# Hybrid attention and gMLP block on one core: the split of two turned blocks one step up, and the product with the gate on VectorE

## The chip, the cores and the metric

The kernel runs on one core of one Trainium2 chip. The metric is the device time of one execution in microseconds (us); the number compared is the median of several runs. Besides the runs there is one profiled execution, from which all rows below are taken. PE is the matrix engine (TensorE), PEld its weight load, ACT is ScalarE, DVE is VectorE, POOL is GpSimd, and SP is the engine that issues most of the DMAs.

## The reference

One layer of a decoder trunk over 1024 positions of width 1024, in float32:

```python
h      = rms_norm(x, pre_norm)
proj   = h @ w_in            # q, k, v, gate_a, u_b, v_b, gate_b, mg_a, mg_b
o_a    = sliding_window_attention(q, k, v, sinks, rel_bias)   # 16 heads of 64, 2 kv heads, window 128
y_a    = (o_a * silu(gate_a)) @ w_branch_a
o_b    = spatial_gating(gelu(u_b), gelu(v_b), ...)            # chunks of 128
y_b    = (o_b * silu(gate_b)) @ w_branch_b
merged = sigmoid(mg_a) * y_a + sigmoid(mg_b) * y_b
x      = x + rms_norm(merged @ w_out, post_norm)
```

The change concerns `o_a * silu(gate_a)`. In `sliding_window_attention` each block of 128 queries attends the 128 keys of its own block up to the diagonal and the keys of the block before it above the diagonal. With a sink the softmax has one more column, which is dropped afterwards.

## The kernel before, in words

**Matrix products.** Every float32 product is made of three products of rounded operands: high half by high half, high half by low half, low half by high half. The high half is a rounding copy (ACT writes it), the low half is the value minus the high half (POOL or DVE). The projection of `h` goes through 24 pairs `n` of 128-column slices of `w_in`: pairs 0 to 15 are in turn a Q pair (a slice of q and the slice of gate_a that belongs to it) and an M pair (merge gates), pairs 16 to 23 are U pairs. Each pair is computed by a seven-product scheme (products 1 to 7 of quarters); a product is 12 matmuls of 128x512. The order is written out by hand: pair `n` has seven steps `s`, and in step `s` PE runs the product `STEPS[s]` of (2, 6, 7, 5, 1, 3, 4), where product 1 is already that of pair n+1. The low halves of the weights are POOL's (`left_lo`, L1816), the high halves ACT's (`left_hi`, L1363 to L1382), four sums per pair are POOL's too (L1881 to L1890). ACT copies the products 1, 6 and 5 out of PSUM (L1396, L1408, L1422, semaphore `ev_ok`); products 6, 5 and 3 of the same bank wait for these copies.

**Attention between the products.** A pair `p` of heads (8 in all) is spread over 22 steps, k = 0 to 21, where k = 7(n-1)+s - 14p; the next pair of heads begins 14 steps after the one before, so its steps 0 to 7 coincide with the steps 14 to 21 of the one before. `attention_all(n, s)` lists, for the current step, first the older pair of heads and then the newer. Each engine has its own loop over n and s and calls `attend(p, k)` for these; PE does so in the middle of its product, after 6 of the 12 matmuls, the others ahead of the step's other work (`after(n, s)`).

Eight blocks of 128 queries start at steps 0, 1, 3, 4, 6, 7, 9, 10: scores on PE (L1049), mask, bias and maximum on DVE (L2131, L2134), exponentials on ACT (L1572), a step later division on ACT (L1580) and a turn of 32x32 squares on DVE (L2143). Two blocks make a couple c = 0 to 3. `couple_at(k, lag)` gives the couple with 3c + lag = k:

- lag 3, SP: `prob_away` stores the probabilities of the couple in DRAM (L665), behind the turn.
- lag 5, SP: `prob_back` loads them back turned as a whole, in four DMAs (L673), behind the store (`prob_out`) and behind POOL's low half of the couple before (`pool_own`, L671), because there is one buffer `turned_in`.
- lag 7, ACT, behind the step's other work: `turned_hi` copies the high half into `pt_pack` (L1589). It waits for the four loads (`prob_in`) and for the values of the couple before (`values_ok`).
- lag 8, POOL, ahead of the step's other work: low half (L1859), then the mask that makes `pt_prev` (L1864, `pt_ok`).
- lag 9, PE: `values` multiplies with v into a half of `ps_m` (L1072), behind `pt_ok` and `oadd_ok` of two couples before. In this step the values stand ahead of the scores.
- lag 10, ACT and DVE: ACT copies one half of the heads' values to the other partitions (L1604, L1605), DVE adds the other half to it in `o_tmp` (L2149, L2150, `oadd_ok`).
- lag 11, POOL: `o_tmp` times the gate, into the gate (L1873, `og_ok`). ACT's next copy into `o_tmp` waits for `og_ok`.
- steps 15 and 21, SP: a half of the gated rows is stored in `ga_d` (L686).

In the middle of the heads (p = 3, step 11) SP loads the k of the second kv head over the first (`load_k(1)`, L693, four DMAs). These stand in SP's queue behind `prob_back` of couple 2. PE's first scores of p = 4 wait for them (`k_in`).

After the pairs three 1024x1024 products follow (branch A, branch B, output).

Of the kernel before, what the change touches and what calls it, by code (L numbers as in the profile page):

```python
# [142 lines left out]
def build(nc, x, rel_bias, pre_norm, post_norm, w_in, sinks, sgu_ln_g, sgu_ln_b,  # L143
# [6 lines left out]
    ALU = mybir.AluOpType  # L150
# [19 lines left out]
    with ExitStack() as ctx:  # L170
# [3 lines left out]
        def sem(name):  # L174
            return ctx.enter_context(nc.semaphore(name))
# [118 lines left out]
        gt_ok, gate_ok = sem("gt_ok"), sem("gate_ok")  # L294
# [7 lines left out]
        otmp_ok, oadd_ok, og_ok = sem("otmp_ok"), sem("oadd_ok"), sem("og_ok")  # L302
# [76 lines left out]
        o_tmp = soft[:, 2 * SOFT_W + 512:2 * SOFT_W + 768]  # L379
# [3 lines left out]
        def gate_w(p, h):  # L383

            return gate[:, 0:HALF] if h == 0 else gate[:, (p % 2 + 1) * HALF:(p % 2 + 2) * HALF]
# [109 lines left out]
        def attention_all(n, s):  # L495

            k = 7 * (n - 1) + s
            p = k // 14
            last = [(p - 1, k % 14 + 14)] if 1 <= p <= HEAD_PAIRS and k % 14 + 14 < LAST_STEP else []
            return last + ([(p, k % 14)] if 0 <= k and p < HEAD_PAIRS else [])  # L500

        def blocks_at(k, lag):

            return [i for i, t in enumerate(BLOCK_AT) if t + lag == k]

        def couple_at(k, lag):

            return [j for j in range(4) if 3 * j + lag == k]

        @block.sync  # L510
        def _(sp):
# [164 lines left out]
            def attend(p, k):  # L676
                for c in couple_at(k, 3):
                    prob_away(4 * p + c)
                for c in couple_at(k, 5):
                    prob_back(4 * p + c)  # L680
                if k == 11 and p + 1 < HEAD_PAIRS:
                    load_bias(p + 1)
                if k in (15, 21):
                    h = k // 21
                    sp.wait_ge(og_ok, 4 * p + 2 * h + 2)
                    sp.dma_start(ga_d[bass.ds(p, 1), :, h * HALF:(h + 1) * HALF].rearrange("a p s -> p (a s)"),  # L686
                                 gate_w(p, h)).then_inc(ga_out[h], 16)
# [527 lines left out]
        def _(act):  # L1215
# [367 lines left out]
            def turned_hi(j):  # L1583
                act.wait_ge(prob_in, 64 * (j + 1))
                if j:
                    act.wait_ge(values_ok, 2 * j)
                else:
                    act.wait_ge(v_out, 16)
                nc.scalar.activation(pt_pack[:, 0:512], turned_in, ACT.Copy).then_inc(turn_hi, 1)  # L1589

            def attend(p, k):
                for blk in blocks_at(k, 1):
                    norm(p, blk)
                for blk in blocks_at(k, 0):
                    exps(p, blk)
                if k == 2 and p + 1 < HEAD_PAIRS:
                    act.dma_start(*skew(p + 1)).then_inc(bias_out, 16)
                for g in couple_at(k, 10):
                    gg = 4 * p + g
                    act.wait_ge(values_ok, 2 * gg + 2)  # L1600
                    if gg:
                        act.wait_ge(og_ok, gg)
                    o = ps_m[:, (g % 2) * 512:(g % 2 + 1) * 512]
                    nc.scalar.activation(o_tmp[0:64, :], o[64:128, 0:256], ACT.Copy)  # L1604
                    nc.scalar.activation(o_tmp[64:128, :], o[0:64, 256:512], ACT.Copy).then_inc(otmp_ok, 1)  # L1605

            def after(n, s):

# [73 lines left out]
            for n in range(1, PAIRS):  # L1682
                for s in range(7):
                    for at in attention_all(n, s):
                        attend(*at)
                    after(n, s)
                    for p, k in attention_all(n, s):
                        for c in couple_at(k, 7):
                            turned_hi(4 * p + c)
            def after_tile(f, i):  # L1690


# [26 lines left out]
        def _(pool):  # L1719
# [44 lines left out]
            for half in range(2):  # L1764
                c = slice(half * HALF, (half + 1) * HALF)
# [80 lines left out]
            def attend(p, k):  # L1846
                if k == 0:
                    if p:
                        pool.wait_ge(exp_ok, 8 * p)
                    else:  # L1850
                        pool.wait_ge(pool_own, 4)
                        pool.wait_ge(vlo_ok, 2)
                    nc.gpsimd.tensor_scalar(neg_s.rearrange("p (b j) -> p b j", b=2)[:, :, 0:2 * SINK_W:2 * SINK_W - 1],
                                            sink_b[:, None, 2 * p:2 * p + 2].to_broadcast([P, 2, 2]), 1.0, 1.0, ALU.mult,
                                            ALU.mult).then_inc(sink_ok, 1)
                for c in couple_at(k, 8):
                    j = 4 * p + c
                    pool.wait_ge(turn_hi, j + 1)
                    nc.gpsimd.tensor_tensor(pt_pack[:, 512:1024], turned_in, pt_pack[:, 0:512].bitcast(f32),  # L1859
                                            ALU.subtract).then_inc(pool_own, 1)  # L1860
                    pool.wait_ge(pool_own, POOL_FRONT + j + 1)
                    if j:
                        pool.wait_ge(values_ok, 2 * j)
                    nc.gpsimd.affine_select(  # L1864
                        out=pt_prev[:, :].rearrange("p (y q) -> p y q", y=8),
                        in_=pt_pack[:, :].rearrange("p (y q) -> p y q", y=8), compare_op=ALU.is_ge, fill=0.0,
                        base=-1, pattern=[[0, 8], [-1, P]], channel_multiplier=1).then_inc(pt_ok, 1)
                for g in couple_at(k, 11):
                    if g == 0:
                        pool.wait_ge(gate_ok, 2 * p + 2)  # L1870
                    part = gate_w(p, g // 2)[:, g % 2 * 256:(g % 2 + 1) * 256]
                    pool.wait_ge(oadd_ok, 4 * p + g + 1)
                    nc.gpsimd.tensor_tensor(part, o_tmp, part, ALU.mult).then_inc(og_ok, 1)  # L1873

            def left_sums_1(n):

# [53 lines left out]
        def _(dve):  # L1930
# [184 lines left out]
            def attend(p, k):  # L2115
                if k == 0:
                    if p == 0:
                        dve.wait_ge(made, MADE_BEFORE)
                    dve.wait_ge(bias_in, 16 * (p + 1))
                for blk in blocks_at(k, 1):  # L2120
                    m2 = slice(blk % 4 * 2, blk % 4 * 2 + 2)
                    dve.wait_ge(exp_ok, 8 * p + blk + 1)
                    nc.vector.reciprocal(inv_den[:, m2], row_sum[:, m2]).then_inc(inv_ok, 1)  # L2123
                for blk in blocks_at(k, 0):
                    s = 8 * p + blk
                    dve.wait_ge(scores_ok, s + 1)
                    if s >= 2:
                        dve.wait_ge(exp_ok, s - 1)
                    bank = ps_s[s % 2]
                    if blk > 0:  # L2130
                        own.link(nc.vector.copy_predicated(blocks(bank)[:, :, 1, :], before_i, blocks(bank)[:, :, 0, :]))  # L2131
                    for h in range(2):
                        bias = h * 256 + (0 if blk else P)
                        ins = nc.vector.tensor_tensor_reduce(  # L2134
                            out=neg_w(blk, h)[:, 1 - h:1 - h + P], in0=bank[:, h * 256 + P:(h + 1) * 256], in1=bias_t[:, bias:bias + P],
                            scale=-HEAD_DIM ** -0.5, scalar=sink_b[:, 2 * p + h:2 * p + h + 1], op0=ALU.add, op1=ALU.min,
                            accum_out=neg_max[:, head(blk, h)])
                    ins.then_inc(scores_used, 1)
                for blk in blocks_at(k, 1):
                    dve.wait_ge(prob_ok, 8 * p + blk + 1)  # L2140
                    for h in range(2):
                        w = prob_w(8 * p + blk, h)
                        ins = nc.vector.transpose(w, w)  # L2143
                    ins.then_inc(turn_ok, 1)
                for g in couple_at(k, 10):
                    gg = 4 * p + g
                    dve.wait_ge(otmp_ok, gg + 1)
                    o = ps_m[:, (g % 2) * 512:(g % 2 + 1) * 512]
                    own.link(nc.vector.tensor_tensor(o_tmp[0:64, :], o[0:64, 0:256], o_tmp[0:64, :], ALU.add))  # L2149
                    nc.vector.tensor_tensor(o_tmp[64:128, :], o[64:128, 256:512], o_tmp[64:128, :],  # L2150
                                            ALU.add).then_inc(oadd_ok, 1)

            def u_mix(n):

# [440 lines left out]
```

## Time and profile before

| | |
|---|---|
| median of 3 runs | 937.08 us |
| lowest and highest | 934.45, 937.41 us |
| the profiled execution | 935.18 us |
| its span, first to last instruction | 933.4 us |
| granted TensorE clock, mean | 0.997 of full speed |
| PE busy | 891.1 us |
| DVE busy | 620.2 us |
| POOL busy | 537.3 us |
| ACT busy | 507.7 us |

The span is what the trace covers; the execution's own time is 1.8 us more. The attention runs from some 150 us to 590 us. One period of 14 steps (one pair of heads) takes 50.2 us there; the pair p = 5, whose step 0 lies at 414.9 us, is the one that is followed below. Busy time alone doesn't say what sets the end: a wait that ends last does.

### The profile page before, as it was taken

Reading aid. Unit: us, or ns where it says so; the run is one execution under the profiler, and the core shown is the slowest. Engines: PE = TensorE matmul, PEld = TensorE weight load, DVE = VectorE, ACT = ScalarE, POOL = GpSimd, SP = SyncE. Lnnn points to the kernel's source line nnn. Section 1 sums busy time; section 2 is a strip of 40 time slices with the busy share of each in tenths; the row PEclk is TensorE's granted clock in tenths of the full one; section 3 lists DMA queues with packets and bytes.
Section 4 is the critical chain, followed back from the end, with each engine's and each line's share of the span. In section 5 each row is a group of like instructions: output and inputs, shape, how many; then the busy total and the mean of one; then the engine's idle time right before and its main releaser. Section 6 shows DMA issues by size and latency. Waiting matters only on the chain.

```text
span 933.4 us, 12475 instructions
## 1 busy us (share of the span) xinstructions
PE 891.1 (95%) x4204; PEld 740.2 (79%) x4204; DVE 620.2 (66%) x1135; ACT 507.7 (54%) x982; POOL 537.3 (58%) x395
## 2 busy tenths in 40 slices
PE   9999999999999998899999989999999999999997
PEld 8888888877777776677777778878888888888886
DVE  6776794544454553445454567879769968989968
ACT  6654356756757574657667674434353534434553
POOL 3564237687888776687788867645444042042226
PEclk9999999999999999999999999999999999999999
DMA  8885746444444457555444454552359560235004
GB/s 299 198 198 159 249 134 182 140 114 129 111 125 117 134 137 158 175 122 146 119 121 108 121 180 134 173 154 91 113 182 382 188 219 22 93 133 225 0 1 181
DMA packets 199184, 139.29 MB, mean 149 GB/s; under 512 B 91320, under 2 KB 164048, under 8 KB 198992
## 3 DMA queue, kind: packets, MB, share of 16 engines
q1 hardware_dynamic: 196880, 135.05, 48.7%
q10 hardware_dynamic: 2240, 3.43, 1.0%
q8 instruction: 34, 0.56, 0.3%
q14 instruction: 30, 0.25, 0.1%
HBM read 98.06 MB, written 43.54 MB: 152 GB/s over the span
## 4 chain that ended last, share of the span: by engine, by line
PE 54%; POOL 23%; issue 9%; DVE 4%; ACT 4%; DMA 3%; SPq 1%; POOLq 0%; DVEq 0%; ACTq 0%
PE acc L1032 13%; PE acc L1204 11%; PE acc L885 9%; POOL w_lo L1816 8%; PE ps_m L1204 7%; PE ps_t L1204 7%; POOL pt_pack L1859 4%; POOL pt_prev L1864 3%; DMA raw<-in_w_in 3%; PE acc L975 2%; POOL sums L1881 2%; POOL sums L1882 2%; POOL gate L1873 1%; PE ps_m L1072 1%; POOL sums L1888 1%
## 5 line engine op out<-in xcount | busy, mean ns | idle before, releaser
L1032 PE MATMUL acc<-mv,w_hi 128*128 128x512 f32 x1344 | 346.7, 391 | 1.2 <-ACT ev L1408 0.7
L1032 PEld LDWEIGHTS acc<-mv,w_hi 128*128 128x128 f32 x1344 | 247.5, 188 | 48.8 <-ACT w_hi L1363 1.1
L1032 PE MATMUL acc<-mv,w_lo 128*128 128x512 f32 x672 | 180.8, 391 | 0.0
L1816 POOL TENSOR_TENSOR w_lo<-sums,w_hi 128x1024 fp32r<-128x1024 f32 x48 | 117.2, 2444 | 71.4 <-ACT w_hi L1370 42.2
L1032 PEld LDWEIGHTS acc<-mv,w_lo 128*128 128x128 f32 x672 | 126.7, 189 | 27.5
L1816 POOL TENSOR_TENSOR w_lo<-raw,w_hi 128x1024 fp32r<-128x1024 f32 (+1 forms) x48 | 94.4, 1967 | 37.1 <-ACT w_hi L1363 27.8
L1572 ACT ACTIVATE soft<-soft,neg_max 128x129 f32<-128x129 f32 x128 | 50.5, 396 | 92.6 <-DVE neg_max L2134 68.0
L1204 PE MATMUL acc<-right,left 128*128 128x512 f32 x432 | 98.7, 389 | 0.0
L1204 PEld LDWEIGHTS acc<-right,left 128*128 128x128 f32 x432 | 81.0, 188 | 17.2 <-DVE left L2194 0.4
L1859 POOL TENSOR_TENSOR pt_pack<-soft,pt_pack 128x512 fp32r<-128x512 f32 x32 | 44.8, 1401 | 52.2 <-ACT pt_pack L1589 52.2
L885 PE MATMUL acc<-mv 128*128 128x512 f32 x288 | 69.5, 395 | 0.0
L2149 DVE TENSOR_TENSOR soft<-ps_m,soft 64x256 f32<-64x256 f32 x32 | 13.3, 417 | 84.1 <-ACT soft L1605 84.1
L1204 PE MATMUL ps_t<-right,left 128*128 128x512 f32 x288 | 67.2, 389 | 0.0
L1204 PE MATMUL ps_m<-right,left 128*128 128x512 f32 x288 | 67.2, 389 | 0.0
L1204 PEld LDWEIGHTS ps_m<-right,left 128*128 128x128 f32 x288 | 54.1, 188 | 11.2
L1204 PEld LDWEIGHTS ps_t<-right,left 128*128 128x128 f32 x288 | 54.1, 188 | 11.2
L885 PEld LDWEIGHTS acc<-mv 128*128 128x128 f32 x288 | 53.5, 189 | 11.0 <-POOL mv L1766 0.2
L2143 DVE STREAM_TRANSPOSE soft<-soft 128x128 f32<-128x128 f32 x128 | 32.3, 291 | 42.1 <-ACT soft L1580 41.9
L1580 ACT ACTIVATE soft<-soft,inv_den 128x128 f32<-128x128 f32 x128 | 44.2, 393 | 29.4 <-DVE inv_den L2123 29.3
L2131 DVE COPY_PREDICATED ps_t<-before,ps_t 128x256 f32<-128x256 int32 x56 | 24.0, 429 | 51.7 <-PE ps_t L1049 50.7
L1072 PE MATMUL ps_m<-pt_pack,v_st 128*128 128x256 f32 x128 | 26.7, 300 | 31.3 <-POOL pt_prev L1864 31.3
L1072 PEld LDWEIGHTS ps_m<-pt_pack,v_st 128*128 128x128 f32 x128 | 19.5, 188 | 41.7 <-POOL pt_prev L1864 41.0
(282 smaller groups left out, 1664.5 us busy)
## 6 DMA issues: line engine op xcount, KB each, us to landing
raw<-in_w_in SPq DMA_DIRECT2D x56, 512.0 KB, 5.6
prob_d<-soft SPq DMA_DIRECT2D x32, 256.0 KB, 3.4
soft<-prob_d SPq DMA_DIRECT2D x128, 64.0 KB, 2.7
ht_d<-sums SPq DMA_DIRECT2D x8, 512.0 KB, 4.8
mix_d<-mix_b SPq DMA_DIRECT2D x8, 512.0 KB, 3.9
ga_d<-gate SPq DMA_DIRECT2D x16, 256.0 KB, 3.6
tb<-tb_d SPq DMA_DIRECT2D x4, 1024.0 KB, 5.4
ub<-mix_d SPq DMA_DIRECT2D x7, 512.0 KB, 3.4
```

The costliest lines, as they stand in the source:

```text
L885: ins = nc.tensor.matmul(acc[b][:, hf * HALF:(hf + 1) * HALF], left, right, start=(m < 2), stop=(m >= 46), skip_group_check=True)
L975: ins = nc.tensor.matmul(acc[b][:, hf * HALF:(hf + 1) * HALF], (w_lo if x == 2 else w_hi)[:, w], right, start=(m < 2), stop=(m >= 46), ski ...
L1032: ins = nc.tensor.matmul(bank, (w_lo if y == 2 else w_hi)[:, left + k * P:left + (k + 1) * P], right[:, (OPW if y == 1 else 0) + k * HALF: ...
L1072: ins = nc.tensor.matmul(o, v_st[:, v0:v0 + P], pt[:, y * 512:(y + 1) * 512].rearrange("p (x c) -> p x c", x=4)[:, heads, :], start=(kb == ...
L1204: ins = nc.tensor.matmul(bank, l[:, c:c + P], r[:, (OPW if y == 1 else 0) + k * HALF:(OPW if y == 1 else 0) + (k + 1) * HALF], start=(m == ...
L1572: ins = nc.scalar.activation(exp_w(s, h), neg_w(blk, h), ACT.Exp, scale=-1.0, bias=neg_max[:, head(blk, h)], accum_out=row_sum[:, head(blk ...
L1580: ins = nc.scalar.activation(w, w, ACT.Copy, scale=inv_den[:, head(blk, h)])
L1816: nc.gpsimd.tensor_tensor(w_lo[:, c], src, w_hi[:, c].bitcast(f32), ALU.subtract).then_inc(wlo_ok, 1)
L1859: nc.gpsimd.tensor_tensor(pt_pack[:, 512:1024], turned_in, pt_pack[:, 0:512].bitcast(f32), ALU.subtract).then_inc(pool_own, 1)
L1864: nc.gpsimd.affine_select(out=pt_prev[:, :].rearrange("p (y q) -> p y q", y=8), in_=pt_pack[:, :].rearrange("p (y q) -> p y q", y=8), comp ...
L2131: own.link(nc.vector.copy_predicated(blocks(bank)[:, :, 1, :], before_i, blocks(bank)[:, :, 0, :]))
L2143: ins = nc.vector.transpose(w, w)
```

## The change

ACT makes the high half of a couple in step 3c + 6, inside `attend`, where it was in step 3c + 7 behind everything else of the step. POOL makes the low half and the mask in step 3c + 7, where it was 3c + 8. The product with the gate goes from POOL (step 3c + 11) to DVE (step 3c + 10, right behind the addition of the values). SP stores the gated halves in steps 14 and 20, where it was 15 and 21.

```diff
--- before.py
+++ after.py
@@ -680,8 +680,8 @@
                     prob_back(4 * p + c)
                 if k == 11 and p + 1 < HEAD_PAIRS:
                     load_bias(p + 1)
-                if k in (15, 21):
-                    h = k // 21
+                if k in (14, 20):
+                    h = k // 20
                     sp.wait_ge(og_ok, 4 * p + 2 * h + 2)
                     sp.dma_start(ga_d[bass.ds(p, 1), :, h * HALF:(h + 1) * HALF].rearrange("a p s -> p (a s)"),
                                  gate_w(p, h)).then_inc(ga_out[h], 16)
@@ -1603,6 +1603,8 @@
                     o = ps_m[:, (g % 2) * 512:(g % 2 + 1) * 512]
                     nc.scalar.activation(o_tmp[0:64, :], o[64:128, 0:256], ACT.Copy)
                     nc.scalar.activation(o_tmp[64:128, :], o[0:64, 256:512], ACT.Copy).then_inc(otmp_ok, 1)
+                for c in couple_at(k, 6):
+                    turned_hi(4 * p + c)
 
             def after(n, s):
 
@@ -1684,9 +1686,6 @@
                     for at in attention_all(n, s):
                         attend(*at)
                     after(n, s)
-                    for p, k in attention_all(n, s):
-                        for c in couple_at(k, 7):
-                            turned_hi(4 * p + c)
             def after_tile(f, i):
 
 
@@ -1853,7 +1852,7 @@
                     nc.gpsimd.tensor_scalar(neg_s.rearrange("p (b j) -> p b j", b=2)[:, :, 0:2 * SINK_W:2 * SINK_W - 1],
                                             sink_b[:, None, 2 * p:2 * p + 2].to_broadcast([P, 2, 2]), 1.0, 1.0, ALU.mult,
                                             ALU.mult).then_inc(sink_ok, 1)
-                for c in couple_at(k, 8):
+                for c in couple_at(k, 7):
                     j = 4 * p + c
                     pool.wait_ge(turn_hi, j + 1)
                     nc.gpsimd.tensor_tensor(pt_pack[:, 512:1024], turned_in, pt_pack[:, 0:512].bitcast(f32),
@@ -1865,12 +1864,6 @@
                         out=pt_prev[:, :].rearrange("p (y q) -> p y q", y=8),
                         in_=pt_pack[:, :].rearrange("p (y q) -> p y q", y=8), compare_op=ALU.is_ge, fill=0.0,
                         base=-1, pattern=[[0, 8], [-1, P]], channel_multiplier=1).then_inc(pt_ok, 1)
-                for g in couple_at(k, 11):
-                    if g == 0:
-                        pool.wait_ge(gate_ok, 2 * p + 2)
-                    part = gate_w(p, g // 2)[:, g % 2 * 256:(g % 2 + 1) * 256]
-                    pool.wait_ge(oadd_ok, 4 * p + g + 1)
-                    nc.gpsimd.tensor_tensor(part, o_tmp, part, ALU.mult).then_inc(og_ok, 1)
 
             def left_sums_1(n):
 
@@ -2149,6 +2142,11 @@
                     own.link(nc.vector.tensor_tensor(o_tmp[0:64, :], o[0:64, 0:256], o_tmp[0:64, :], ALU.add))
                     nc.vector.tensor_tensor(o_tmp[64:128, :], o[64:128, 256:512], o_tmp[64:128, :],
                                             ALU.add).then_inc(oadd_ok, 1)
+                    dve.wait_ge(oadd_ok, gg + 1)
+                    if g == 0:
+                        dve.wait_ge(gate_ok, 2 * p + 2)
+                    part = gate_w(p, g // 2)[:, g % 2 * 256:(g % 2 + 1) * 256]
+                    nc.vector.tensor_tensor(part, o_tmp, part, ALU.mult).then_inc(og_ok, 1)
 
             def u_mix(n):
 
```

## Rows read from the trace of the kernel before

**Rows 1.** The page: PE's busy time, and the chain that ended last, by engine.
```profile
PE 891.1 (95%) x4204; PEld 740.2 (79%) x4204; DVE 620.2 (66%) x1135; ACT 507.7 (54%) x982; POOL 537.3 (58%) x395
...
PE 54%; POOL 23%; issue 9%; DVE 4%; ACT 4%; DMA 3%; SPq 1%; POOLq 0%; DVEq 0%; ACTq 0%
```

**Rows 2.** The waits, whole span: who waited for whom, us in total, times, longest.
```profile
PE ps_m L1072 <- POOL pt_prev L1864: 31.3, 23, 2.9
...
SPq L671 <- POOL pt_pack L1859: 144.1, 31, 7.4
```

**Rows 3.** One window: start:end, length; busy PE, PEld, DVE, ACT, POOL; granted clock; DMA.
```profile
414.93:465.15 50.22, 46.38 (x232) 38.61 (x231) 24.33 (x84) 32.44 (x84) 40.16 (x30) 1.00 0.48 129
```

**Rows 4.** PE's timeline: start us, length us, group, [idle before <-releaser].
```profile
423.64 1.53 PE L1032 MATMUL acc<-mv,w_hi 128*128 128x512 f32 x6
...
430.00 0.50 PE L1072 MATMUL ps_m<-pt_pack,v_st 128*128 128x256 f32 x2 [1.62 <-POOL pt_prev L1864]
...
442.04 1.98 PE L1032 MATMUL acc<-mv,w_hi 128*128 128x512 f32 x8
...
444.76 1.52 PE L1032 MATMUL acc<-mv,w_hi 128*128 128x512 f32 x6
447.47 0.74 PE L1072 MATMUL ps_m<-pt_pack,v_st 128*128 128x256 f32 x4 [1.18 <-POOL pt_prev L1864]
...
458.62 0.50 PE L1072 MATMUL ps_m<-pt_pack,v_st 128*128 128x256 f32 x2 [1.04 <-POOL pt_prev L1864]
...
468.33 0.40 PE L1072 MATMUL ps_m<-pt_pack,v_st 128*128 128x256 f32 x2
```

**Rows 5.** ACT's timeline, the same stretch.
```profile
440.33 1.04 ACT L1377 ACTIVATE w_hi<-sums 128x1024 fp32r<-128x1024 f32 x1
...
444.26 0.61 ACT L1589 ACTIVATE pt_pack<-soft 128x512 fp32r<-128x512 f32 x1
...
454.86 0.60 ACT L1422 ACTIVATE c<-acc 128x512 f32<-128x512 f32 x1
```

**Rows 6.** POOL's timeline, the same stretch.
```profile
441.45 2.41 POOL L1816 TENSOR_TENSOR w_lo<-sums,w_hi 128x1024 fp32r<-128x1024 f32 x1 [3.08 <-ACT w_hi L1377]
444.95 1.30 POOL L1859 TENSOR_TENSOR pt_pack<-soft,pt_pack 128x512 fp32r<-128x512 f32 x1 [1.09 <-ACT pt_pack L1589]
```

**Rows 7.** SP's timeline: DMA issues; and the landing times of L673 by its source.
```profile
354.94 1.24 SPq L693 DMA_DIRECT2D k_lo<-k_d  x2
...
425.94 0.32 SPq L665 DMA_DIRECT2D prob_d<-soft  x1
432.34 2.60 SPq L673 DMA_DIRECT2D soft<-prob_d  x4
...
DMA to landing us min/median/max: 2.4/2.7/4.4
```

**Rows 8.** DVE: a turn of couple 3 (timeline); then by source, ns min/median/max.
```profile
457.31 0.51 DVE L2143 STREAM_TRANSPOSE soft<-soft 128x128 f32<-128x128 f32 x2 [0.76 <-ACT soft L1580]
...
L2150 DVE TENSOR_TENSOR soft<-ps_m,soft x32: 427/427/429, 197.6 to 584.5; 64x256 f32<-64x256 f32 x32
...
L2173 DVE TENSOR_TENSOR ub<-ub,ev x7: 691/692/1108, 560.6 to 677.2; 128x512 f32<-128x512 f32 x7
...
L2173 DVE TENSOR_TENSOR sums<-sums,ev x1: 2901/2901/2901, 696.5 to 696.5; 128x512 f32<-128x512 f32 x1
```

**Rows 9.** POOL: the product with the gate by source, ns min/median/max.
```profile
L1873 POOL TENSOR_TENSOR gate<-soft,gate x32: 722/738/1706, 200.8 to 586.1; 128x256 f32<-128x256 f32 x32
```

**Rows 10.** PE around the reload of k: timeline, and the window behind it.
```profile
361.30 0.30 PE L1049 MATMUL ps_t<-k_hi,q_st 128*128 128x128 f32 x1 [3.02 <-issue]
...
361.77 1.00 PE L1032 MATMUL acc<-mv,w_hi 128*128 128x512 f32 x2
...
366.17 0.40 PE L1072 MATMUL ps_m<-pt_pack,v_st 128*128 128x256 f32 x2
...
361.30:366.10 4.80, 4.80 (x16) 3.89 (x17) 2.00 (x7) 2.12 (x6) 2.61 (x2) 0.64 1.28 229
```

## The prediction

> **What bounds the kernel now.** I read the page's busy times first: PE is busy 95% of the span, and the chain that ended last is PE for 54% and POOL for 23% [rows 1]. So PE is the bound, and what POOL has in that chain is time in which PE stood still for it. The table of waits names it: PE's matmuls on the values waited 31.3 us for POOL's mask, in 23 of the 32 couples [rows 2]. Read as a period: 14 steps take 50.22 us, in which PE is busy 46.38, so 3.84 us are lost in each of the eight pairs of heads [rows 3]. PE's timeline shows where: three waits, 1.62 us before couple 3, 1.18 before couple 0, 1.04 before couple 1, and none before couple 2, at 468.33 [rows 4]. Their sum is 3.84 us, the whole of the loss. No other engine is full in the period: ACT 32.4 us, DVE 24.3, POOL 40.2 [rows 3].
>
> Why is the mask late? Take couple 0. PE's product of that step starts at 444.76; six matmuls at 2.72/12 us each (twelve matmuls from 442.04 to 444.76) end at about 446.1, and the values start only at 447.47 [rows 4]. POOL began the low half at 444.95 and had waited 1.09 us for ACT's high half [rows 6]; from there to PE's first matmul it is 2.52 us. ACT began the high half at 444.26, behind the step's other work [rows 5]. The chain is place in ACT's queue, high half 0.6, low half 1.3, mask 1.1, values.
>
> **High half, low half and mask earlier.** ACT now makes the high half of couple 0 in step 6, ahead of the weight copy that started at 440.33 [rows 5]. The loads must have landed. The store of couple 0 is issued at 425.94, and the four loads at 432.34, so a store and its wait take at most 6.4 us; the loads take 2.6 us to issue, and one lands in 2.7 (median), so the four are in 4.65 us after the first issue, at 437.0 [rows 7]. That is 3.3 us ahead of 440.33; PE's 1.62 us wait at 430.0, which goes, leaves 1.7 us, and the product on DVE (below) another 0.7 or so less. So the high half is done about 3.9 us earlier than now (440.9 against 444.9). POOL, idle for 3.08 us before 441.45 [rows 6], does low half and mask from 440.9 to 443.4: PE wants them at 446.1, 2.7 us later. The wait of couple 0 goes.
>
> What stands behind them is pushed: on ACT the weight copy and what follows come 0.5 us later, on POOL the low half of weights at 441.45 starts at 443.4. It is for a product that PE reaches some three steps on, near 451; harmless. Couple 1: its loads wait for POOL's low half of couple 0 (SP waited 144.1 us in all for that, 31 times [rows 2]); this now ends at 442.2 rather than 446.3, so they are in at 446.9, and ACT comes to them only behind the exponentials of scores that PE begins at 447.1, at about 449.8. POOL then has mask, weights (2.4), weights (2.4), sums (2.6) in a row from 440.9, so low half 450.8 to 452.1 and mask to 453.3, against PE at 456.3: 2.9 us spare. Couple 2 follows at 461.1 to 462.3 against 466. Couple 3 is the tight one. Its turn ends at 457.8 now [rows 8]; with 0.45 for the product ahead of it and less 1.18, the store is issued at 457.1, +6.4 +4.65 lands at 468.2. ACT meets this high half in step 15, ahead of the exponentials and of the copy out of PSUM (`ev_ok`) for which PE waits at the start of step 17. That start is at 423.64 in this period [rows 4], so 473.86 in the next, 471.6 without the two waits. High half, division, exponentials and copy are 2.5 us, so the loads may land until 469.1: 0.9 us spare with the longest store seen, 1.7 with one of 5.6.
>
> All three waits go: -31.3 us.
>
> **The product with the gate.** POOL loses 32 products of 0.738 us [rows 9]: its load per period goes from 40.2 to 37.2 us, of 46.4 then. Nothing waited for it but ACT's next copy and the store, so this alone is worth nothing on the path; it makes room. DVE gains 32. The trace doesn't show this operation on DVE. From below: half of the 128x512 addition with both inputs in SBUF, 0.35 us; from above: the same operation on the last U pair took 2.90 us [rows 8]. I take 0.42, that of the 256-column addition it stands behind [rows 8], plus 0.03 for the added wait on its own result: 0.45 x 32 = 14 us of a DVE that has 22 us free in a period. Behind it on DVE stand a reciprocal (so ACT's division, the turn and the store), and the additions of the products. On the path: 0 at 0.45; at 2.9 the turn of couple 3 is 2.5 us late against 0.9 to 1.7 spare, so 0.8 to 1.6 us per pair of heads, 6 to 13 us in all, and this is the top of this term. The stores of the gate one step up stand behind the loads of couple 3 and before the store of couple 1 in SP's queue; DVE's product is done some 0.4 us behind the addition, before the turn that the next store waits for. Nothing.
>
> The 0.69 and the 2.90 us are the same operation of the same size: the second ran beside POOL's long low halves. The Trainium skill (SBUF — State Buffer, "SBUF: two separate sides") says that a VectorE instruction with two SBUF inputs and a GpSimd instruction exclude each other for a whole instruction. By that rule each product can wait for a POOL instruction of up to 2.4 us, and the change brings it into the stretch in which POOL never pauses; the rows above agree that such a thing happens, and it is the third rival below.
>
> **The reload of k.** In the middle of the heads PE waits 3.02 us for the second k [rows 10]. Its four DMAs stand in SP's queue behind the loads of couple 2, and these behind POOL's low half of couple 1. That comes 5.3 us earlier (452.1 against 457.4 in the period followed), so the last two DMAs, issued from 354.94 [rows 7], go out some 5 us earlier and land near 356. PE gets there, with two waits of 1.18 and 1.04 us gone, at 355.9. The wait shrinks to 0 to 0.5: -3.0. Behind the wait the granted clock was 0.64 over 4.8 us, so part of it at the level of 1.2 GHz, and twelve matmuls from 361.77 to 366.17 took 4.40 us instead of 2.72 [rows 4, 10]. Without the wait that is another -1.7. From the other side both may stay: 0.
>
> **The sum.** The profiled execution took 935.18 us (span 933.4 and 1.8 around it). 935.18 - 31.3 - 3.0 - 1.7 = 899.2. It lies 1.9 us below the median of the runs, so 901.1; I add 1 us for what is left of the k wait and small new ones: **902 us**. As a check, eight periods at PE's busy time instead of 50.2 give 8 x 3.84 = 30.7, and the rest of the 31.3 is one longer wait (2.9 in place of 1.2) behind the reload of v, less the one of the 24 waits that is missing.
>
> **The rivals.**
>
> 1. The reload of k doesn't gain, since its landing (beside two weight loads) or SP's queue sets it: 4.7 us stay, 906. For it: landings vary by microseconds, and the store before it is as long as 6.4 us; against it: its issue is bound to POOL's low half, which moves by 5 us.
>
> 2. Nothing is gained: the turned loads land so late that ACT, waiting, hands the high half over no sooner, 936. For it: the loads hang on two DMA trips. Against: ACT's copy at 444.26 shows no wait [rows 5], and the landing comes 7 us ahead of it (437.0).
>
> 3. The product collides with POOL on DVE as above, or one of the three kinds of wait stays: 8 x 1.0 to 8 x 1.6 are 8 to 13 us, 909 to 915. For it: the 2.90 us row. Against: by my order of POOL's work above, the products find it mostly in sums, low halves and masks of 1.1 to 1.3 us, not in the 2.4 us ones.
>
> 4. Slower: ACT stands at the high half of couple 3 in step 15 with exponentials and the copy out of PSUM behind it, and PE stops at its product in step 17, in every pair of heads. This starts to cost from 0.9 us beyond the landing worked out, and eats the 36 us gained when it is 36/8 = 4.5 us per pair more, so from 5.4 us beyond it: two DMA trips of 16.5 us rather than 11. Then, at a lateness of 6.5, it costs 8 x 5.6 = 45 us, 946. For it: before, this wait stood behind all other work of its step, where it could hold up nothing of that step, and now it stands ahead. Against: no load of these took longer than 4.4 us, and the store and its wait are already taken at 6.4 [rows 7].
>
> **How the numbers follow.** Forecast (898 to 905) 0.60; rival 1 (905 to 908) 0.14; rival 3 (908 to 920) 0.12; better than forecast by other waits that go, 0.04; rival 2 0.04; rival 4 0.06. Faster by over 0.3% (2.8 us, about what the runs here can tell from none): 0.60 + 0.14 + 0.12 + 0.04 = 0.90; within 0.3%: 0.04; slower: 0.06. The range 897 to 914 leaves out part of rival 3 and rivals 2 and 4, under 2 in 10.
>
> **What would show it right or wrong.** In the profile of the changed kernel the row of PE waiting for the mask has gone or is under 2 us; a period of 14 steps takes about 46.4 us, and POOL is busy 37 of it; the product on DVE reads 0.42 to 0.5 us, with a maximum that tells rival 3; PE's wait at the first scores of the fifth pair of heads is under 0.5 us and no slow stretch follows. PE's waits for ACT's copies out of PSUM, which take no part in the 3.84 us of a period now, must stay small: if they come to over 8 us, my spare time for couple 3 is wrong. If POOL's mask is early but the period stays over 48 us, the bound was not the mask.

## The result, and the profile after

| kernel | median, us (lowest to highest) | ratio to before, 95% interval |
|---|---|---|
| before, same chip | 935.77 (932.98 to 937.41) | |
| changed | 912.32 (909.63 to 913.36) | 0.9748 [0.9712, 0.9783] |

The changed kernel is 2.5% faster. The forecast was 902, so it was 10 us too low: the time lies inside the range given (897 to 914), but outside the forecast's own band (898 to 905); it is where rival 3 stood (909 to 915). The profiled execution took 909.63 us with a span of 907.9, 25.5 below the 933.4 of before. All rows of "after" are from it.

The page: busy times, and the chain that ended last, by engine, against [rows 1].

```profile
PE 888.9 (98%) x4204; PEld 741.4 (82%) x4204; DVE 652.0 (72%) x1167; ACT 506.7 (56%) x982; POOL 511.8 (56%) x363
...
PE 55%; issue 10%; DVE 10%; POOL 9%; ACT 8%; DMA 6%; SPq 3%; ACTq 0%; DVEq 0%; POOLq 0%
```

POOL's share of the chain fell from 23% to 9%; DVE's rose from 4 to 10 and ACT's from 4 to 8. PE's waits over the whole span answer to [rows 2]:

```profile
PE acc L1032 <- ACT c L1422: 5.3, 4, 2.9
PE ps_t L1049 <- DVE q_st L2089: 2.6, 1, 2.6
PE acc L1032 <- DVE ev L2082: 2.5, 1, 2.5
PE acc L1032 <- ACT ev L1408: 1.4, 2, 0.9
```

There is no wait for the mask any more, where there were 31.3 us. In its place stand 11.8 us in eight waits for ACT and DVE. The period that was followed before the change (pair p = 5, 14 steps, columns as in [rows 3]):

```profile
395.77:441.39 45.62, 45.62 (x231) 38.86 (x230) 27.72 (x86) 31.58 (x84) 36.32 (x25) 1.00 0.48 132
```

It takes 45.62 us instead of 50.22, and PE does not stop in it; POOL has 36.32 us of work (I had said 37). But not all periods are like this one. The distances from one pair of heads' first scores to the next (before, then after, in us): 46.4, 50.2, 50.2, 53.4, 53.6, 50.2, 50.2 and 43.7, 45.7, 46.8, 48.6, 50.1, 45.6, 46.7. The seven sum to 27.3 us gained; behind the last first scores, 1.8 are given back. Two places lost most. The fifth pair still waits for its k, and the clock falls behind that (PE's timeline, and a window with the columns of [rows 3], against [rows 10]):

```profile
345.68 0.30 PE L1049 MATMUL ps_t<-k_hi,q_st 128*128 128x128 f32 x1 [2.62 <-DVE q_st L2089]
...
348.54 2.16 PE L1032 MATMUL acc<-mv,w_hi 128*128 128x512 f32 x6
...
345.68:350.48 4.80, 4.80 (x16) 3.89 (x17) 2.60 (x8) 1.94 (x5) 2.39 (x2) 0.64 1.26 234
```

(The releaser named, DVE's q_st, had long been done; the last loads of k were issued at 339.49.) And in the last pair of heads PE stands for 2.89 and 2.47 us, where DVE also has the sums of the weights and other work of the U pairs:

```profile
528.92 1.62 PE L1032 MATMUL acc<-mv,w_hi 128*128 128x512 f32 x6 [2.89 <-ACT c L1422]
...
544.47 3.62 PE L1032 MATMUL acc<-mv,w_hi 128*128 128x512 f32 x8 [2.47 <-DVE ev L2082]
```

The second of these can be followed on POOL and DVE. Directly behind the product with the gate stands an instruction that the change does not touch (`ub` times `c`), and behind this the addition (L2082) for which PE waits:

```profile
540.62 2.44 POOL L1815 TENSOR_TENSOR w_lo<-sums,w_hi 128x1024 fp32r<-128x1024 f32 x1 [1.82 <-ACT w_hi L1377]
...
540.40 0.42 DVE L2149 TENSOR_TENSOR gate<-soft,gate 128x256 f32<-128x256 f32 x1
540.74 2.87 DVE L2171 TENSOR_TENSOR ub<-ub,c 128x512 f32<-128x512 f32 x1
543.64 0.69 DVE L2082 TENSOR_TENSOR ev<-acc,ev 128x512 f32<-128x512 f32 x1
```

The product itself is short here (0.42 us), but behind it the next instruction begins after POOL's low half and takes 2.87 us. With no product ahead of it (e5 below) it begins 0.2 us before POOL's and takes 0.69:

```profile
533.91 0.69 DVE L2173 TENSOR_TENSOR ub<-ub,c 128x512 f32<-128x512 f32 x1
```

The experiments below split the same way. With the move and the product on VectorE directly behind its addition (changed, e3, e4, e6) this instruction takes 2.5 to 2.9 us, and PE waits 1.9 to 3.0 for the addition; with the move and the product elsewhere (e1, e5, e10, e11, e12) it takes 0.69, and PE waits 0.5 at most. What set the 2.89 us was not followed.

The product on VectorE, by source (ns min/median/max), which the forecast had at 420 (and 30 for its wait):

```profile
L2149 DVE TENSOR_TENSOR gate<-soft,gate x32: 424/1016/1366, 196.6 to 560.5; 128x256 f32<-128x256 f32 x32
```

19 of the 32 take over 1.0 us, among them couple 3's in all eight pairs of heads: it runs beside the end of one of GpSimd's long low halves of the weights. The one at 417.35, shown below, took 1.03 us beside this:

```profile
415.69 2.41 POOL L1815 TENSOR_TENSOR w_lo<-sums,w_hi 128x1024 fp32r<-128x1024 f32 x1 [2.43 <-ACT w_hi L1370]
```

### The profile page after: what moved, and what is told of

The parts are those of the page before. It is cut to its first block, busy times and chain, and to the rows that moved or that the text cites. A ratio compares the mean times of both kernels' runs of the same rounds, so it can differ in the third digit from the quotient of the medians.

```text
span 907.9 us, 12475 instructions
## 1 busy us (share of the span) xinstructions
PE 888.9 (98%) x4204; PEld 741.4 (82%) x4204; DVE 652.0 (72%) x1167; ACT 506.7 (56%) x982; POOL 511.8 (56%) x363
## 3 DMA queue, kind: packets, MB, share of 16 engines
q1 hardware_dynamic: 196880, 135.05, 50.1%
## 4 chain that ended last, share of the span: by engine, by line
PE 55%; issue 10%; DVE 10%; POOL 9%; ACT 8%; DMA 6%; SPq 3%; ACTq 0%; DVEq 0%; POOLq 0%
PE acc L1032 14%; PE acc L1204 11%; PE acc L885 10%; PE ps_m L1204 7%; PE ps_t L1204 7%; POOL w_lo L1815 4%; PE acc L975 2%; DMA soft<-prob_d 2%; DMA prob_d<-soft 2%; POOL pt_pack L1858 2%; SPq L673 2%; ACT soft L1572 1%; DVE gate L2149 1%; DMA raw<-in_w_in 1%; POOL pt_prev L1863 1%
## 5 line engine op out<-in xcount | busy, mean ns | idle before, releaser
L1572 ACT ACTIVATE soft<-soft,neg_max 128x129 f32<-128x129 f32 x128 | 50.3, 394 | 45.4 <-DVE neg_max L2127 45.1
L1580 ACT ACTIVATE soft<-soft,inv_den 128x128 f32<-128x128 f32 x128 | 44.0, 392 | 51.2 <-DVE inv_den L2116 51.2
L1858 POOL TENSOR_TENSOR pt_pack<-soft,pt_pack 128x512 fp32r<-128x512 f32 x32 | 41.8, 1306 | 38.0 <-ACT pt_pack L1589 38.0
L885 PEld LDWEIGHTS acc<-mv 128*128 128x128 f32 x288 | 53.2, 188 | 11.8 <-ACT mv L1237 0.5
L2127 DVE CUSTOM_DVE_ANT_0 soft<-ps_t,bias_t,sink_b 128x128 f32<-128x128 f32 x128 | 39.9, 349 | 2.2 <-issue 0.2
L1821 POOL TENSOR_TENSOR left<-w_a,left 128x1024 fp32r<-128x1024 f32 x7 | 18.6, 2677 | 37.4 <-ACT left L1511 37.4
L1821 POOL TENSOR_TENSOR left<-s_buf,left 128x1024 fp32r<-128x1024 f32 x6 | 15.2, 2553 | 42.9 <-ACT left L1511 42.9
```

Source lines behind the costliest of these rows:

```text
L885: ins = nc.tensor.matmul(acc[b][:, hf * HALF:(hf + 1) * HALF], left, right, start=(m < 2), stop=(m >= 46), skip_group_check=True)
L1572: ins = nc.scalar.activation(exp_w(s, h), neg_w(blk, h), ACT.Exp, scale=-1.0, bias=neg_max[:, head(blk, h)], accum_out=row_sum[:, head(blk ...
L1580: ins = nc.scalar.activation(w, w, ACT.Copy, scale=inv_den[:, head(blk, h)])
L1821: ins = nc.gpsimd.tensor_tensor(left[f % 2][:, OPW:2 * OPW][:, c], left_src(f // 7, ORDER[f % 7])[:, c], left[f % 2][:, c].bitcast(f32), A ...
L2127: ins = nc.vector.tensor_tensor_reduce(out=neg_w(blk, h)[:, 1 - h:1 - h + P], in0=bank[:, h * 256 + P:(h + 1) * 256], in1=bias_t[:, bias:b ...
```

## The experiments

| kernel | what it is | median, us | ratio, 95% interval |
|---|---|---|---|
| e1_move | high half, low half, mask up one step; product on GpSimd | 901.51 | 0.9647 [0.9630, 0.9665] |
| e2_product | product on VectorE, gate's stores one step up; nothing else | 951.07 | 1.0188 [1.0159, 1.0218] |
| e3_psum | changed, product reads PSUM and one SBUF tile | 904.29 | 0.9682 [0.9663, 0.9701] |
| e4_kload | changed, k reloaded earlier | 909.94 | 0.9740 [0.9714, 0.9766] |
| e5_late | changed, product one step later | 901.11 | 0.9639 [0.9608, 0.9669] |
| e6_twice | e3 with the product made twice | 908.21 | 0.9720 [0.9691, 0.9748] |
| e7_end | e1, high half at the end of step 6 | 902.98 | 0.9667 [0.9635, 0.9698] |
| e8_front | before, high half ahead in step 7 | 912.82 | 0.9771 [0.9738, 0.9804] |
| e9_alone_late | e2 with the late product, stores as before | 941.38 | 1.0066 [1.0041, 1.0091] |
| e11_ahead | e5, product at the front of its step | 902.61 | 0.9664 [0.9645, 0.9683] |
| e10_vhalf | e5, second half of v reloaded later | 899.74 | 0.9634 [0.9613, 0.9654] |
| e12_vhalf_pool | e1, the same | 900.29 | 0.9634 [0.9618, 0.9651] |

Each ratio is to runs of the kernel before on the same chip (medians 935.03, 934.51 and 934.86 in the three sets: e1 to e4, e5 to e8, e9 to e12). Between two sets the ratios are the safer guide: the changed kernel is 10.8 us above e1 by the medians, and 9.5 by the ratios (0.0101 of 935 us).

**The two halves of the change, each alone.** e1 takes the product's lines back:

```diff
-                    dve.wait_ge(oadd_ok, gg + 1)
-                    ...
-                    nc.vector.tensor_tensor(part, o_tmp, part, ALU.mult).then_inc(og_ok, 1)
+                for g in couple_at(k, 11):
+                    ...
+                    nc.gpsimd.tensor_tensor(part, o_tmp, part, ALU.mult).then_inc(og_ok, 1)
```

e2 is the reverse: high half, low half and mask stay where they were, and the product goes to VectorE, with the gate's stores one step up.

> The move alone: high half, low half and mask one step up as in the changed kernel, the product with the gate stays on POOL one step behind the addition. Theory A (the mask was late because of its place in ACT's queue; POOL's load did not matter): all of PE's waits for the mask go here too, the time is that of the changed kernel, 910 to 915 us. Theory B (POOL's 26 us of products had a part in it, because POOL now never pauses between steps 7 and 12): some of the waits for the mask stay, 1 us or so in one or two couples of each pair of heads, 918 to 928 us. Theory C (the product costs more on VectorE than it saves on POOL, since it collides there): this kernel is faster than the changed one, 904 to 908 us.

> The product on VectorE alone, high half, low half and mask where they were before. Theory A: nothing, 933 to 938 us, and PE waits for the mask 29 to 32 us as before. Theory B: POOL, freed of 26 us, has the mask earlier where the product stood ahead of its weights: 5 to 12 us gained, 924 to 931 us. Theory C: slower than before by some us, 938 to 944 us.

The move alone brings 33.5 us, all that the forecast had for the whole change. The product on VectorE costs 16 us by itself, and 9.5 to 11 beside the move. e2's waits of PE show a part of it:

```profile
PE ps_m L1072 <- POOL pt_prev L1864: 39.4, 23, 2.4
```

Same 23 waits as before, 8.1 us longer [rows 2]. That is half of the loss. The other half is PE's own time: it is busy 899.9 us instead of 891.1, at a mean granted clock of 0.986 instead of 0.997; in the two periods from 370.56 on it is 0.94 and 0.97.

**The product without the second SBUF input.** The sums are written into PSUM and the product reads them there:

```diff
-                    nc.vector.tensor_tensor(part, o_tmp, part, ALU.mult).then_inc(og_ok, 1)
+                    nc.vector.tensor_tensor(part, o[:, 0:256], part, ALU.mult).then_inc(og_ok, 1)
```

> The changed kernel with the sums of the values written into PSUM, and the product taking its first input from there, so that it has one input in SBUF instead of two (PE's wait for a free half moves behind the product). If the long products (0.42 to 1.37 us in the trace) come from two SBUF inputs beside a POOL instruction, all 32 now read 0.42 us. Theory D (these collisions make VectorE late, then ACT's copies out of PSUM, and so the 8 us in which PE now waits for ACT and VectorE): the time falls by 4 to 8 us to 904 to 908 us. Theory A: they have room, at most 1 to 2 us, 910 to 912 us.

```profile
L2149 DVE TENSOR_TENSOR gate<-ps_m,gate x32: 423/424/426, 196.9 to 555.5; 128x256 f32<-128x256 f32 x32
```

All 32 take the same 0.42 us, and 8.0 of the 10.8 us come back (by the ratios 6.2 of 9.5). The Trainium skill (SBUF — State Buffer, "SBUF: two separate sides") says that a VectorE instruction with two SBUF inputs and a GpSimd instruction that reads SBUF exclude each other for a whole instruction. The traces agree: up to 1.37 us with two inputs in SBUF, 0.42 in 32 of 32 with one of them in PSUM.

**Length, or place?** e6 puts a second product of 0.41 us in front of e3's, written into the scratch tile. e5 keeps the changed kernel's product as it is, but makes it in the following step, at the end of its own pair's attention work:

```diff
+                for g in couple_at(k, 11):
+                    gg = 4 * p + g
                     dve.wait_ge(oadd_ok, gg + 1)
                     ...
```

> The kernel whose sums are written into PSUM (904.3 us, product 0.42 us each time) with the product made twice, first into the scratch tile and then in place: so VectorE's queue carries 0.85 us per couple, still with one input in PSUM each. Theory L (the length in VectorE's queue is what costs, whatever makes it long): 0.42 us more of length is what the collisions added in the changed kernel to within a third, so it comes to 908 to 912. Theory S (the collision costs since it also holds up GpSimd, whose low halves and masks PE needs; VectorE has time to spare): length by itself costs nothing, 904 to 906.

> The changed kernel with VectorE's product taken out of its place directly behind the addition and put at the end of the attention work of the next step (behind that step's scores and turns); the gate's stores are issued one step later again, as before the change. Length, inputs and number of the products are the same. Theory P (place): the product costs because it stands ahead of the reciprocal and the scores of the same step, on which ACT's exponentials wait. Then this comes to 903 to 907 us. Theory L (length): in either step the product takes 1.0 us in the median (against 0.42 with one input in PSUM) and the same in-order queue carries it ahead of PE's next additions; then it stays at 909 to 914. The changed kernel is 912.3, the move alone 901.5.

e6 loses 3.9 us to e3 by length alone (3.6 by the ratios; the slowest run of e3 is 905.90, the fastest of e6 907.20). e5's product is in sum no shorter than the changed kernel's, and yet e5 is as fast as the move alone:

```profile
L2151 DVE TENSOR_TENSOR gate<-soft,gate x32: 380/525/1604, 198.5 to 551.9; 128x256 f32<-128x256 f32 x32
```

(28.8 us in all, against 28.0 in the changed kernel.) So products of the same total length cost nothing at one place and 10 us or so at another. The expectation put e5's product behind the scores of its step; for couples 1 to 3 that is not so, since the older pair's work comes first: it stands ahead of the next pair's scores, but behind the reciprocals of the step before. DVE's timelines tell what stands behind it. Changed kernel, then ACT's next work, around couple 3 of one pair of heads:

```profile
416.44 0.42 DVE L2142 TENSOR_TENSOR soft<-ps_m,soft 64x256 f32<-64x256 f32 x1 [2.79 <-ACT soft L1605]
416.89 0.43 DVE L2143 TENSOR_TENSOR soft<-ps_m,soft 64x256 f32<-64x256 f32 x1
417.35 1.03 DVE L2149 TENSOR_TENSOR gate<-soft,gate 128x256 f32<-128x256 f32 x1
418.31 0.15 DVE L2116 RECIPROCAL inv_den<-row_sum 128x2 f32<-128x2 f32 x1
...
418.49 0.69 ACT L1580 ACTIVATE soft<-soft,inv_den 128x128 f32<-128x128 f32 x2 [2.08 <-DVE inv_den L2116]
```

The same stretch with the late product:

```profile
411.75 0.43 DVE L2143 TENSOR_TENSOR soft<-ps_m,soft 64x256 f32<-64x256 f32 x1
412.21 0.17 DVE L2116 RECIPROCAL inv_den<-row_sum 128x2 f32<-128x2 f32 x1
413.13 0.51 DVE L2136 STREAM_TRANSPOSE soft<-soft 128x128 f32<-128x128 f32 x2 [0.76 <-ACT soft L1580]
413.56 0.38 DVE L2151 TENSOR_TENSOR gate<-soft,gate 128x256 f32<-128x256 f32 x1
...
412.40 0.70 ACT L1580 ACTIVATE soft<-soft,inv_den 128x128 f32<-128x128 f32 x2 [1.14 <-DVE inv_den L2116]
```

In the changed kernel ACT stands 2.08 us for the reciprocal, with the product ahead of it; in e5, 1.14. Couples 2 and 3 of one pair of heads end in steps in which the next pair's blocks already run, and the next pair's reciprocals follow in DVE's queue (seven of the eight pairs have a next one). ACT's waits for the reciprocal, summed over each trace, go the way the times go: 31.6 us in e1 and e5 (901.5 and 901.1 us), 37.6 in e11 (902.6), 39.4 in e3 (904.3), 46.6 in e6 (908.2), 51.2 in the changed kernel (912.3).

That leaves a rival: which instructions collide differs too. In e5 couple 3's product takes 0.38 us in seven of eight pairs, and the product that makes the gate (`gate_mul`, below) takes at its second place 0.69 us in six of eight, where the changed kernel has 1.3 to 1.8. This last row alone does not set the time: in e1, as fast as e5, it takes 1.4 to 1.9 in seven of eight. The additions of the same step also stand behind the changed kernel's product, and no run separated them from the reciprocal.

The two kernels also differ in a step of the gate's stores; in the changed kernel's trace the gate's store was issued from 418.41 for 0.42 us, and the turned block's at 419.75, as soon as the turn was made. So the gate's store held nothing there, but no run separated the two edits.

> The kernel with the late product (901.1 us), the product still in the next step but at its front, ahead of the reciprocal. Theory P: it is again between the addition and the reciprocal, as in the changed kernel, so 908 to 914. Theory N (what helped was the step between, in which the collision happens with another GpSimd instruction, or the later store): 900 to 904.

e11 took the time that theory N named, but it was a weak test. For couples 1 to 3 the following step begins with the ending pair's work anyway, so its place is the same as e5's; only couple 0 gets a reciprocal behind its product. The result (1.5 us above e5, intervals overlapping) decides neither theory for the rest.

**The product alone, late.**

> The kernel before (high half, low half and mask unmoved) with the product on VectorE at the late place: behind the scores and turns of the next step. The same edit directly behind the addition took 951 us. Theory P (the 16 us were the reciprocal's delay, handed on through ACT's division and exponentials to the high half at the end of ACT's step and so to the mask): now nothing is delayed, 931 to 937. Theory C (they were the collisions with GpSimd, which last as long at the late place): 945 to 953.

Between the two theories: 9.7 of e2's 16 us go, 6.5 stay. The trace shows a cost that neither the prediction nor the expectations had in the account: `gate_mul`, which makes the gate from its tanh on VectorE (L2109 before, L2103 in e2 and e9), reads two SBUF tiles as well. Before, e2, e9:

```profile
L2109 DVE SCALAR_TENSOR_TENSOR gate<-c x8: 683/864/908, 163.6 to 518.0; 128x512 f32<-128x512 f32 x8
```
```profile
L2103 DVE SCALAR_TENSOR_TENSOR gate<-c x8: 681/2623/2640, 163.7 to 532.8; 128x512 f32<-128x512 f32 x8
```
```profile
L2103 DVE SCALAR_TENSOR_TENSOR gate<-c x8: 681/2909/2924, 164.3 to 523.3; 128x512 f32<-128x512 f32 x8
```

Pushed by a few tenths of a microsecond, it begins beside GpSimd's low half of the weights and lasts until that is done. In e9, DVE and then POOL:

```profile
421.38 2.91 DVE L2103 SCALAR_TENSOR_TENSOR gate<-c 128x512 f32<-128x512 f32 x1
...
421.34 2.40 POOL L1816 TENSOR_TENSOR w_lo<-sums,w_hi 128x1024 fp32r<-128x1024 f32 x1
423.70 2.84 POOL L1816 TENSOR_TENSOR w_lo<-raw,w_hi 128x1024 fp32r<-128x1024 f32 x1
```

That is 1.8 to 2.0 us more in six of the eight pairs of heads. How much of e2's and e9's loss it is was not tried by itself. Two kernels further down speak against most of it, as long as the mask is early: with the product on GpSimd, e7 has this row at 2.3 to 2.5 us in five of eight pairs and e8 at 1.9 to 2.5 in six, and e7 is 1.5 us above e1, with intervals that overlap.

**What the move needs.** e7 moves ACT's high half from behind the attention work of step 6 to the end of step 6 (`turned_hi` behind `after(n, s)`); e8 takes the kernel before and moves only the high half, from the end of step 7 to behind its attention work.

> The move alone (901.5 us), with the high half still in step 6 but at the end of ACT's work of that step instead of behind its attention work. Theory A1 (what the move brought is the step; within it the place is free, since the end of step 6 is still some 3 us ahead of the end of step 7): 900 to 903. In it ACT no longer stands at the turned loads of couple 3 with the copy out of PSUM behind it, so PE's waits for ACT's copies (5.3 us in the move alone) may shrink by up to 2. Theory A2 (the place counts: GpSimd gets the high half about 1 us later and stands before its own low halves of weights): mask waits come back at 0.3 to 1 us each, 907 to 925.

> The kernel before with one edit: the high half is made behind ACT's attention work of step 7 instead of at the end of step 7; low half, mask, product (on GpSimd) and stores are where they were. The high half is then done some 2 us earlier, but GpSimd takes it at its old place, where it stood 1.09 us for it. Theory Q (each link of the chain is bound by the one before, so GpSimd starts 1.09 us earlier and the waits of 1.62, 1.18 and 1.04 us of a pair of heads shrink to about 0.5, 0.1 and 0): 31.3 us of waits become 4 to 9, 908 to 914. Theory R (GpSimd's own place is as late: the work ahead of it ends no sooner once the high half does not hold it): less than half goes, 920 to 930.

The place within step 6 is worth little. e8's 912.8 is as foretold: eight mask waits of 0.9 us stay, and that of k with them.

```profile
PE ps_m L1072 <- POOL pt_prev L1863: 7.5, 8, 1.9
PE ps_t L1049 <- issue: 2.6, 1, 2.6
```

So one line moved on ACT, without GpSimd or VectorE, brings 22 of the 33.5 us. It is the delay of ACT's queue that made the mask late.

**The reload of k, and that of v.** e4 issues the four loads of k ahead of the loads of couple 2 (`load_k(1)` ahead of `prob_back`). e10 and e12 issue the second half of v's reload behind the step's two weight loads:

```diff
-                        for half in range(2):
+                        for half in (0,):
                         ...
+                    if n == FIRST_U - 7 and s == 6:
+                        for half in (1,):
```

> The changed kernel with the reload of k for the second kv head issued ahead of the turned loads of couple 2 in SP's queue, so that it waits for the last scores of the fourth pair of heads alone. If the 2.6 us for which PE stands before the fifth pair of heads, and the slow twelve matmuls behind it, come from the place in SP's queue: the wait goes, 4.3 us less, 907 to 909 us. If the transfer itself, or the scores, set it: no change, 911 to 914 us.

> The kernel with the late product (901.1 us), and the second half of the reload of v issued behind the two loads of weights of that step, not ahead of them: it is first read six steps after the first half. ACT stood 3.4 us for these weights, PE 1.96 us behind it, and 12.5 us of PE at a lower clock follow. If the 0.5 MB ahead of the weights set their landing, they land some 1.5 us earlier, PE's wait falls under 1 us: 898 to 900. If the landing is set otherwise, 901.

> The move alone (product on GpSimd, 901.5 us) with the same split of the reload of v. Same expectation, 898 to 900, and against the run with the product on VectorE it tells which engine is the better one for the product once its place does not matter: within 1 us if neither is on the path.

In e4 the wait at the fifth pair's first scores is gone; in the same profile the waits for ACT's copies are 5.6 and 4.6 us instead of 5.3 and 1.4. Its 909.9 us lie between the two expectations, and its ratio is within the changed kernel's interval. So with ACT and DVE late, the earlier load bought PE little or nothing. In e10 the fifth period takes 48.2 us instead of e5's 50.3. Over the whole kernel e10 and e12 have the lowest medians of all, 899.7 and 900.3, but their intervals overlap those of e5 and e1: the product on either engine, once it stands where nothing waits, comes to the same.

## Why the prediction was right or wrong, point by point

- **PE bound, the mask late by ACT's place in the queue, three waits per pair of heads: right.** No mask wait is left in the changed kernel, and e8 shows that the high half's place was the first link. The gain in an undisturbed period was 4.6 us, 0.8 more than the 3.84 that PE's waits summed to: PE's busy time [rows 3] fell as well, from 46.38 to 45.62 us. Why it did, no run shows.
- **The mask's spare time: too wide.** For couple 0 I had 2.7 us. GpSimd's mask in the changed kernel runs from 423.74 for 1.09 us, and PE's values begin at 425.09, 0.3 us later. With the late product (mask from 417.96, values at 421.40) it is 2.4 us. I had taken ACT's and DVE's work to come forward as PE's waits went. It hung on the product and the reciprocal instead.
- **The product, 0.45 us and 0 on the path: this is the step that failed.** It took 0.88 us in the mean, and cost 9.5 to 11 us (901.5 without it on VectorE, 912.3 with it). The upper bound of the term, 6 to 13 us, and rival 3 held this size, and its cause, collision with GpSimd; the range held the measured time only because its top left room for them. But the way to the cost was another. I priced the late turn of couple 3; the reciprocal, which I named as standing behind the product and then did not price, stood later by the product's length, and ACT's division with it (51.2 us of waits instead of 31.6). The next instructions of VectorE itself I left out altogether: one of them, pushed by 0.42 us, took 2.87 us and cost PE 2.47. The argument against rival 3, that the products mostly meet GpSimd's 1.1 to 1.3 us instructions, was true of couples 0 to 2 and wrong for couple 3, which met the 2.4 us ones in all eight pairs.
- **What the lateness cost, and where.** Not a wait in each period, as rival 3 had it (8 to 13 us as 8 times 1.0 to 1.6), but few large ones: k's reload, and the last pair of heads.
- **The reload of k: wrong in the changed kernel, right in e1 and e5.** Its issue hangs on GpSimd's low half of couple 1, as I said. The changed kernel issued k's first loads at 338.3 and waited 2.62 us; e5, whose fifth pair began 3.9 us earlier (341.8 against 345.7), did not wait. So rival 1 happened along with rival 3: 2.6 us, and the slow stretch behind it, at a granted clock of 0.64, as in [rows 10].
- **Rival 4 (ACT stands at the high half, the copies out of PSUM are late): the mechanism is there, small.** PE's waits for these copies come to 6.7 us, under the 8 that I had set as the sign.
- **The sum, and some luck in it.** The sum said 899.2 for the profile and 901.1 for the median; e1 gives 901.05 and 901.51. The terms for the mask (one wait of 1.1 us left) and for k (no wait) came out one by one. Two others were off and cancelled: PE's busy time fell by 5.6 us (891.1 to 885.5), where only 1.7 were counted, and PE's waits for ACT and DVE grew by 4.5 us (1.3 to 5.8), where I had 1.

What stays open: e6, with the same length at the same place as the changed kernel (0.84 against 0.88 us), has a median 4 us lower. By the ratios it is 2.6 us, and the intervals overlap, so it may be less. If it is real, unequal collisions (`gate_mul` takes 1.71 against 1.45 us at its second place, in the mean of the last seven) and GpSimd's side of them were not separated; nor was the step of the gate's stores in e5.

## What to carry to other kernels

Price an instruction put into an in-order queue by what the next entries release, not by that engine's idle time: here 32 products that cost some 10 us behind an addition cost nothing one step later, at the same total length. Where VectorE reads two SBUF tiles beside a busy GpSimd, read the maximum of every such instruction, also of those that the change does not touch, since a shift of tenths of a microsecond can move one of them into a collision of 2 us (in the last pair of heads here, PE paid 2.5 us for one). When a change is two edits, run each alone first: the better kernel here was half of the change.

## What the runs showed of the hardware that was not expected

- A VectorE product of 128x256 with both inputs in SBUF took 0.38 to 0.43 us when no GpSimd instruction ran beside it, and up to 1.97 us (e11) and once 2.62 (e9) when one did; with one input in PSUM, 0.42 us in 32 of 32 (e3).
- GpSimd is held up too: its low half of 2.40 us took 2.84 us behind the collision shown for e9.
- Of two instructions the later one to begin pays most: `ub` times `c` (128x512, both inputs in SBUF) took 0.69 us when it began 0.2 us before GpSimd's low half (e5), and 2.87 us when it began 0.1 us after it (changed); the low half took 2.44 us then, and 2.73 in e5.
- One wait of PE of 2.6 us was followed by 4.8 us at a granted clock of 0.64 (so in part at 1.2 GHz), six matmuls of them in 2.16 us instead of the 1.53 us of [rows 4].
